# Hybrid encoder block on one core: modulation weights in column blocks, the first three w_in slabs as one group, three engines on the token tiles

## What is computed

```python
mod = jax.nn.silu(c) @ w_ada[l] + b_ada[l]                       # w_ada 1024 x 6144
sh1, sc1, gt1, sh2, sc2, gt2 = jnp.split(mod[:, None, :], 6, axis=-1)
h = rmsnorm(x, g_norm1[l]) * (1.0 + sc1) + sh1
x = x + gt1 * mixer_sublayer(h, w_in[l], ...)                    # first: z = h @ w_in, w_in 1024 x 7168
h = rmsnorm(x, g_norm2[l]) * (1.0 + sc2) + sh2
x = x + gt2 * hier_moe(h, ...)                                   # 32 experts, 2 per token
...
return rmsnorm(x, g_final)
```

## Time and profile before

| | us |
|---|---|
| median of 3 runs | 1762.74 |
| profiled execution | 1762.71 |
| its span in the trace | 1760.9 |
| PE busy | 1587.8 (90%) |
| DVE busy | 1336.4 (76%) |
| ACT busy | 682.0 (39%) |
| Pool busy | 339.0 (19%) |
| mean granted TensorE clock | 0.96 |

### The profile page before, as it was taken

The page is one execution under the profiler, slowest core; times in us unless marked ns, Lnnn a source line. Parts: engine busy times, 40 slices in busy tenths (PEclk is TensorE's granted clock), DMA queues, the critical chain, the costliest instruction groups (busy, mean ns, idle before and its releaser), DMA issues.

```text
span 1760.9 us, 21630 instructions
## 1 busy us (share of the span) xinstructions
PE 1587.8 (90%) x7040; PEld 1290.2 (73%) x7040; DVE 1336.4 (76%) x1152; ACT 682.0 (39%) x574; POOL 339.0 (19%) x208
## 2 busy tenths in 40 slices
PE   2799999999999997997989965999999999999981
PEld 2688888888888885775777854788887777777861
DVE  5687869678696878349435446999999999899984
ACT  4401121121111202214213122777776766676762
POOL 1100000000000000000000002255454444345440
PEclk9999999999999998998999975999999999999995
DMA  7413323142232315423426253999999999999945
GB/s 267 142 54 115 107 94 108 60 131 83 84 107 95 107 48 194 128 72 120 132 85 201 101 203 124 348 366 371 373 360 361 361 351 358 359 352 356 370 143 208
DMA packets 167572, 352.07 MB, mean 200 GB/s; under 512 B 17229, under 2 KB 90957, under 8 KB 167542
## 3 DMA queue, kind: packets, MB, share of 16 engines
q1 hardware_dynamic: 150838, 309.71, 49.9%
q0 software_dynamic: 16704, 41.98, 7.9%
HBM read 323.84 MB, written 46.66 MB: 210 GB/s over the span
## 4 chain that ended last, share of the span: by engine, by line
PE 59%; DMA 18%; DVE 13%; issue 4%; ACT 4%; POOL 1%; DVEq 0%; SPq 0%; POOLq 0%; ACTq 0%
PE ps L1220 18%; PE ps L1222 18%; PE ps L1221 18%; DMA e_raw<-in_w_down_dram 15%; DVE e_lo L1148 3%; ACT e_hi L723 2%; DMA xg<-d_h,g_idx 2%; DVE e_lo L1144 2%; PE ps L1276 2%; DVE macc L836 1%; PE ps L1394 1%; PE ps L1342 1%; DVE s L951 1%; DVE conf L942 1%; DVE f_o L1210 1%
## 5 line engine op out<-in xcount | busy, mean ns | idle before, releaser
L1220 PE MATMUL ps<-A_hi,w_hi 128*128 128x512 f32 x1024 | 402.9, 393 | 23.8 <-DVE A_lo L931 13.0
L1221 PE MATMUL ps<-A_lo,w_hi 128*128 128x512 f32 x1024 | 401.0, 392 | 0.0
L1222 PE MATMUL ps<-A_hi,w_lo 128*128 128x512 f32 x1024 | 400.9, 392 | 0.0
L1144 DVE TENSOR_TENSOR e_lo<-e_raw,e_hi 128x2048 fp32r<-128x2048 f32 x136 | 309.0, 2285 | 12.4 <-ACT e_hi L717 10.8
L921 DVE SCALAR_TENSOR_TENSOR conv_acc_b<-glu,colc,conv_acc_b 128x1024 f32<-128x1024 f32 x232 | 298.0, 1285 | 10.4 <-DVE rows L913 0.3
L717 ACT CAST e_hi<-e_raw 128x2048 fp32r<-128x2048 f32 x136 | 259.7, 1912 | 61.3 <-PE ps L1222 56.1
L1220 PEld LDWEIGHTS ps<-A_hi,w_hi 128*128 128x128 f32 x1024 | 194.0, 189 | 66.9 <-issue 17.8
L1221 PEld LDWEIGHTS ps<-A_lo,w_hi 128*128 128x128 f32 x1024 | 194.1, 190 | 40.7 <-issue 0.5
L1222 PEld LDWEIGHTS ps<-A_hi,w_lo 128*128 128x128 f32 x1024 | 193.8, 189 | 40.6
L1220 PE MATMUL ps<-e_hi,xT_hi 128*128 128x512 f32 x528 | 212.6, 403 | 0.0
L1222 PE MATMUL ps<-e_hi,xT_lo 128*128 128x512 f32 x528 | 206.9, 392 | 0.0
(11 more groups left out here) (227 smaller groups left out, 2025.5 us busy)
## 6 DMA issues: line engine op xcount, KB each, us to landing
e_raw<-in_w_gate_dram SPq DMA_DIRECT2D x132, 512.0 KB, 5.5
e_raw<-in_w_up_dram SPq DMA_DIRECT2D x132, 512.0 KB, 12.4
e_raw<-in_w_down_dram SPq DMA_DIRECT2D x66, 1024.0 KB, 14.0
w_raw<-in_w_in_dram SPq DMA_DIRECT2D x56, 512.0 KB, 4.3
stream<-in_w_ada_dram SPq DMA_DIRECT2D x48, 512.0 KB, 5.7
xn<-in_x_dram SPq DMA_DIRECT2D x8, 512.0 KB, 7.0
d_short<-conv_acc_a POOLq DMA_DIRECT2D x8, 512.0 KB, 4.0
d_gate_a<-gate_st POOLq DMA_DIRECT2D x8, 512.0 KB, 2.9
```

What stands on the lines that cost most here:

```text
L1144: v.tensor_tensor(e_lo[:, q, :], e_raw[:, q, :], e_hi[:, q, :].bitcast(F32), ALU.subtract).then_inc(gu_lo, 1)
L1220: t.matmul(dst, st_hi, mv_hi, start=first, stop=False)
L1221: t.matmul(dst, st_hi, mv_lo, start=False, stop=False)
L1222: return t.matmul(dst, st_lo, mv_hi, start=False, stop=last)
```

## The change

It rewrites the start; from slab 7 on the program is the same.

- **Loads.** The eight parameter loads go out on ACT's queue, `c` first. SP issues all eight x tiles, then four tiles of w_ada, then the first three w_in slabs, then the other twelve tiles of w_ada. A tile of w_ada is now 512 rows by 256 columns (four row blocks side by side in a slot, runs of 1 KB): four tiles (two row halves, shift and scale) complete 256 columns of both vectors.
- **Token tiles.** ACT squares tile i and takes the root of tile i-1; Pool scales x (was ACT); ACT copies the even transposed tiles out of PSUM, DVE the odd ones; `junk0` gets a second buffer. ACT starts no scaling and DVE no modulation sum in this loop.
- **Modulation.** DVE sums in pieces of 256 columns, 64 operations in place of 16, shift and scale in turn, each waiting for the one before the last. After each column block PE adds over the partitions (4 products) and DVE forms two columns of a1.
- **h.** Pool makes `hsc` for all eight k (was four) and the A_lo of odd k; DVE the A_lo of even k.
- **w_lo** of slabs 1 and 2 is made by Pool, of slab 0 by DVE.
- **Products.** Slabs 0, 1 and 2 run together: for each channel block k the three slabs' 18 matmuls, with the column sums of the next modulation block behind k = 0, 2 and 4. Then slab 3 and the rest as before; the first channel is written out, the loop runs over 1 to 7.

The diff, cut to its core:

```diff
+        def ada_block(m):
+            kb, kh, q = m // 4, m // 2 % 2, m % 2
+            return w_ada[kh * H:(kh + 1) * H, q * D + kb * MB:q * D + (kb + 1) * MB].rearrange("(k p) n -> p k n", p=P)
 ...
-            for src, r, n in ((conv_b, 0, KB), (conv_a, ROW_CONV_A, KA), (b_conv_b, ROW_BIAS_B, 1), (ln_g, ROW_LN_G, 1),
-                              (ln_b, ROW_LN_B, 1), (g_norm1, ROW_G1, 1), (b_ada[0:2], ROW_SH, 2), (c, ROW_C, 1)):
-                sp.dma_start(prow[r:r + n, :], src).then_inc(s_par, 16)
             for i in range(NT):
                 sp.dma_start(xn[:, i, :], x[i * P:(i + 1) * P, :]).then_inc(x_full[i], 16)
-                for q in range(2):
-                    load_tile(sp, M_ADA1 + 2 * i + q, w_ada[i * P:(i + 1) * P, q * D:(q + 1) * D])
+            def load_ada(m):
+                if m >= 4:
+                    sp.wait_ge(st_free[m % 4], m // 4)
+                sp.dma_start(tile(M_ADA1 + m).rearrange("p (k n) -> p k n", n=MB), ada_block(m)).then_inc(st_full[m % 4], 16)
+            for m in range(4):
+                load_ada(m)
+            for kind in range(3):
+                sp.dma_start(raw3[:, W_SLOT[kind]], slab_in(KINDS[kind], 0)).then_inc(wr_full[W_SLOT[kind]], 16)
+            for m in range(4, 16):
+                load_ada(m)
             sp.wait_ge(s_const, 1)
             sp.dma_start(rows[0:1, :, :], b_ada[2:6].unsqueeze(0)).then_inc(s_rows_in, 16)
-            sp.wait_ge(s_cols, 2)
-            with sp.Fori(0, KT) as ch:
+            def channel(ch, loaded):
                 for kind in range(NK):
                     s = W_SLOT[kind]
-                    held(w_lo_done, ch * NK + (kind - W_BACK[kind] + 1 + CREDIT_SLAB))
-                    sp.dma_start(raw3[:, s], slab_in(KINDS[kind], ch)).then_inc(wr_full[s], 16)
+                    if kind >= loaded:
+                        held(w_lo_done, ch * NK + (kind - W_BACK[kind] + 1 + CREDIT_SLAB))
+                        sp.dma_start(raw3[:, s], slab_in(KINDS[kind], ch)).then_inc(wr_full[s], 16)
                     if kind in (0, 2, 4, 5):
                         q = (0, 2, 4, 5).index(kind)
                         held(st_free[q], ch + M_ADA2 // 4)
                         sp.dma_start(stream[:, q, :], w_ada[bass.ds(ch * P, P), (2 + q) * D:(3 + q) * D]).then_inc(st_full[q], 16)
+            sp.wait_ge(s_cols, 2)
+            channel(0, 3)
+            with sp.Fori(1, KT) as ch:
+                channel(ch, 0)
 ...
-            pool.wait_ge(s_a1, 1)
-            for k in range(1, KT, 2):
-                if k >= 3:
-                    pool.wait_ge(s_hlo, k - 1)
-                g.tensor_scalar(hsc[:, 1, :], xnT[:, k, :], a1[:, k:k + 1], modc[:, 0, k:k + 1], ALU.mult, ALU.add).then_inc(s_hp, 1)
+            for i in range(NT):
+                pool.wait_ge(s_rstd, i + 1)
+                g.tensor_scalar(xn[:, i, :], xn[:, i, :], rstd[:, i:i + 1], None, ALU.mult).then_inc(s_xn, 1)
+            for kind in range(1, 3):
+                pool.wait_ge(w_hi_done, kind + 1)
+                s = W_SLOT[kind]
+                g.tensor_tensor(w_lo[:, s, :], w_raw[:, s, :], w_hi[:, s, :].bitcast(F32), ALU.subtract).then_inc(s_wlo_pool, 1)
+            def h_f32(k):
+                if k % 2 == 0:
+                    pool.wait_ge(s_a1, k // 2 + 1)
+                    if k >= 2:
+                        pool.wait_ge(s_hlo, k // 2)
+                g.tensor_scalar(hsc[:, k % 2, :], xnT[:, k, :], a1[:, k:k + 1], modc[:, 0, k:k + 1], ALU.mult, ALU.add).then_inc(s_hp, 1)
+            pool.wait_ge(s_xTa, NT // 2)
+            pool.wait_ge(s_xTd, NT // 2)
+            for k in range(0, KT, 2):
+                h_f32(k)
+                h_f32(k + 1)
+                pool.wait_ge(s_hp, k + 2)
+                pool.wait_ge(s_hhi, k + 2)
+                g.tensor_tensor(A_lo[:, k + 1, :], hsc[:, 1, :], A_hi[:, k + 1, :].bitcast(F32), ALU.subtract).then_inc(s_hlo_odd, 1)
+                pool.wait_ge(s_hlo_odd, k // 2 + 1)
 ...
+            for src, r, n in ((c, ROW_C, 1), (b_ada[0:2], ROW_SH, 2), (g_norm1, ROW_G1, 1), (conv_b, 0, KB), (conv_a, ROW_CONV_A, KA),
+                              (b_conv_b, ROW_BIAS_B, 1), (ln_g, ROW_LN_G, 1), (ln_b, ROW_LN_B, 1)):
+                act.dma_start(prow[r:r + n, :], src).then_inc(s_par, 16)
 ...
+            def xT_even(i):
+                act.wait_ge(s_xT, i + 1)
+                a.copy(xnT[:, :, i * P:(i + 1) * P], ps[:, i % 2, :].rearrange("p (k n) -> p k n", k=KT)).then_inc(s_xTa, 1)
 ...
             for i in range(NT):
                 act.wait_ge(x_full[i], 16)
-                a.activation(junk0[:], xn[:, i, :], ACT.Square, accum_out=ss[:, i:i + 1]).then_inc(s_ssq, 1)
-                take_root(0, i)
-                act.wait_ge(s_rstd, i + 1)
-                a.activation(xn[:, i, :], xn[:, i, :], ACT.Copy, scale=rstd[:, i:i + 1]).then_inc(s_xn, 1)
+                if i >= 2:
+                    act.wait_ge(s_ssq, i - 1)
+                a.activation(junk0[:, i % 2, :], xn[:, i, :], ACT.Square, accum_out=ss[:, i:i + 1]).then_inc(s_ssq, 1)
+                if i >= 1:
+                    take_root(0, i - 1)
+                if i >= 3 and i % 2 == 1:
+                    xT_even(i - 3)
+            take_root(0, NT - 1)
             act.sem_inc(act_evac, CREDIT_ACT_EVAC)
             for q in range(2):
                 act.sem_inc(g_free[q], CREDIT_FREE)
-            def split(n, slot, full, before):
-                act.wait_ge(wr_full[slot], full)
-                act.wait_ge(pe_slab, before)
-                a.copy(w_hi[:, slot, :], w_raw[:, slot, :]).then_inc(w_hi_done, 1)
             act.wait_ge(s_cols, 2)
-            for kind in range(2):
+            xT_even(NT - 2)
 ...
+            def mod_sum(kb, kh):
+                tiles = [M_ADA1 + kb * 4 + kh * 2 + q for q in range(2)]
                 for q in range(2):
-                    m = M_ADA1 + 2 * i + q
-                    wait_tile(dve, m)
-                    if i == 0:
-                        ins = v.tensor_scalar(macc1[:, q, :], tile(m), cols[:, i, ROW_C:ROW_C + 1], None, ALU.mult)
-                    else:
-                        ins = v.scalar_tensor_tensor(macc1[:, q, :], tile(m), cols[:, i, ROW_C:ROW_C + 1], macc1[:, q, :],
-                                                     ALU.mult, ALU.add)
-                    step(ins)
-                    dve.sem_inc(st_free[m % 4], 1)
-            dve.sem_inc(s_macc, 1)
-            xT_evac(NT - 1)
-            for kind in range(2):
-                split(W_SLOT[kind], kind + 1)
-            dve.wait_ge(s_modc, 1)
-            step(v.tensor_tensor(modc[:], ps[:, 3, 0:2 * KT].rearrange("p (q k) -> p q k", q=2),
-                                 cols[:, :, ROW_SH:ROW_SC + 1].rearrange("p k q -> p q k"), ALU.add))
-            step(v.scalar_tensor_tensor(a1[:], modc[:, 1, :], 1.0, cols[:, :, ROW_G1], ALU.add, ALU.mult))
-            dve.sem_inc(s_a1, 1)
+                    wait_tile(dve, tiles[q])
+                for j in range(4):
+                    k = kh * 4 + j
+                    ck = cols[:, k, ROW_C:ROW_C + 1]
+                    for q in range(2):
+                        acc = macc1[:, q, kb * MB:(kb + 1) * MB]
+                        src = tile(tiles[q])[:, j * MB:(j + 1) * MB]
+                        if k == 0:
+                            ins = v.tensor_scalar(acc, src, ck, None, ALU.mult)
+                        else:
+                            dve.wait_ge(dv, steps[0] - 1)
+                            ins = v.scalar_tensor_tensor(acc, src, ck, acc, ALU.mult, ALU.add)
+                        steps[0] += 1
+                        ins.then_inc(dv, 1)
+                dve.wait_ge(dv, steps[0])
+                for q in range(2):
+                    dve.sem_inc(st_free[tiles[q] % 4], 1)
+                if kh == 1:
+                    dve.sem_inc(s_macc, 1)
+            def mod_add(kb):
+                dve.wait_ge(s_modc, kb + 1)
+                two = slice(2 * kb, 2 * kb + 2)
+                step(v.tensor_tensor(modc[:, :, two], ps[:, 3, 0:2 * KT].rearrange("p (q k) -> p q k", q=2)[:, :, two],
+                                     cols[:, two, ROW_SH:ROW_SC + 1].rearrange("p k q -> p q k"), ALU.add))
+                step(v.scalar_tensor_tensor(a1[:, two], modc[:, 1, two], 1.0, cols[:, two, ROW_G1], ALU.add, ALU.mult))
+                dve.sem_inc(s_a1, 1)
+            def h_lo_even(k):
+                dve.wait_ge(s_hp, k + 1)
+                dve.wait_ge(s_hhi, k + 1)
+                v.tensor_tensor(A_lo[:, k, :], hsc[:, 0, :], A_hi[:, k, :].bitcast(F32), ALU.subtract).then_inc(s_hlo, 1)
+            mod_sum(0, 0)
+            xT_odd(5)
+            mod_sum(0, 1)
+            xT_odd(7)
+            split(W_SLOT[0], 1)
+            mod_add(0)
+            for kb in range(1, 4):
+                mod_sum(kb, 0)
+                if kb >= 2:
+                    mod_add(kb - 1)
+                else:
+                    h_lo_even(0)
```

(92 more changed lines are left out.)

47 lines of the change are left out of this document (25 added, 22 removed).

## The result

| | before | after |
|---|---|---|
| median of 4 runs each | 1763.25 us | 1784.15 us |
| ratio, 95% interval | | 1.0119, 1.0098 to 1.0141 |
| profiled execution | 1762.71 | 1783.59 |
| its span | 1760.9 | 1781.5 |
| T, start of ACT's first c_sb copy | 101.69 | 123.15 |

The account below looks back on a forecast made before the run. The chain of waits before the first w_in slabs end (T) bounds the kernel, PE being full afterwards. T = 87.6 + 5.5 + 14 = 107.1; + 2.2 - 101.7 = +7.6 us, so 1770 us, range 1751 to 1780.

Parts of the forecast that it names:

- Pool's turns: Before T, Pool's work and DVE's two-input operations exclude each other for whole operations; +14 us, between +9.6 and +18.4.
- late parameters: At the start, parameters share one DMA engine with x, halving their rate; +5.5 us, bounds 0 and +7.
- x tiles: First square to last rstd: ACT sets the pace, Pool's scalings and PE's transposes lie beside it; 18.5 us.
- strict turns: Before T, Pool and DVE alternate, so nearly all Pool's work comes on top; +18.4 us, T = 106.
- Rival 1: Pool and DVE do not block each other in two-input work; 1756 or, with prompt parameters, 1751; chance 0.25.
- one slow start: In the first channel block, PE's first matmuls start 0.43 us apart, not 0.23; +2 us.
- rival 4: PE slow again after pauses between channel blocks, up to three more starts at +2 us; 1776; 0.22 with rival 3.
- DVE's waiting for PE: Before T, 2 to 3 us of Pool's work lie under DVE's waits for PE and cost nothing.
- short sums: Modulation sums over 256 columns on DVE: 0.40 us each, 3.2 for a half block, range 0.34 to 0.48.
- +2.2: Waits of PE after the three-slab group: 1.5 us for slab 3 and 0.7 before slab 5.
- rival 3: Pool and DVE strictly in turns and parameters late; +12.0 us, 1775; chance 0.22 together with rival 4.
- 87.6: T, end of the third slab, if no engine disturbs another and parameters are prompt; range 85 to 90.

Follow-up runs that it names:

- e1: Changed kernel with the eight parameter loads on SP's queue ahead of x, in the new order; 1776.95 us.
- e7: Kernel before with the parameter loads moved to ACT's queue in the new order; 1769.38 us.
- e3: Changed kernel with Pool's scaling of x written with a second operation (plus 0.0) that changes nothing; 1777.30 us.
- e4: Changed kernel with Pool left only the scaling of x ahead of the first products; ACT writes hsc, DVE all A_lo and w_lo; 1773.53 us.
- c2: c1 with parameters on ACT's queue again and all that waits for them moved behind the x tiles; median 1748.59 us, 0.9918 of before.
- e8: e4 plus sixteen Pool operations that read and write SBUF tiles nobody uses; 1785.48 us.
- e9: As e8, but the sixteen extra Pool operations are fills that write SBUF and read nothing; T 111.9, total not given.
- e5: Changed kernel with PE's column sums issued ahead of channel blocks 2 and 4, not behind them; 1781.02 us.
- c1: Changed kernel joining e1 (parameters in before's order), e3, e4 and e5; column blocks and three-slab group kept; median 1757.62 us, 0.9968 of before.

## Why the prediction missed

The forecast of 1770 and the range up to 1780 both lie under the measured 1784. Slower by more than 0.5%, which I had given 0.34, is what came. Pool's turns and the late parameters, the two costs that I named, are there; what failed is the time of the x tiles (Pool's scaling counted as nothing), the size of the parameters' delay, and the slow restarts of PE left out of the sum.

**The account of T.** Forecast 107.1, measured 123.15, 16.0 short. By its own steps:

| step | forecast | measured | miss |
|---|---|---|---|
| first square | 17.0 | 20.86 | 3.9 |
| from it to the last rstd | 18.5 | 23.2 | 4.7 |
| from there to T | 71.6 | 79.05 | 7.4 |

- **Parameters** (+5.5): right in direction, mis-sized: the first square came 9.4 later than before's 11.49. I halved the rate and gave 15 to 16 for the last landing; it was 18.99, more than a halving (flight 15.59 against the 5.95 of the earlier trace rows), and my upper bound of 7 was under it. e1 and e7 show from both sides that the queue makes the delay; how the two queues share the engine no run shows.
- **The x tiles**: the step that failed was "Pool's scalings lie beside it". The prediction gives them no price; the only Pool row that it has is the hsc of 1.20, a two-operation form. The scaling is a one-operation form and took 2.83, longer than ACT's 1.44 a tile. PE's transposes came 2.8 apart, each waiting for Pool, and ACT's copies and roots behind them, so that Pool set the pace. With the two-operation form (e3) the stretch takes 18.1 us, my 18.5, and T falls by 7.0. No row of before shows the form, and I bounded it by nothing.
- **Pool's turns** (+14): right. Against unblocked half blocks (2.99 or 3.25, from e4 and c2) those of after lose 1.8, 4.2, 3.7, 3.5 and 3.7 us, together 16.9; the first 1.8 are beside Pool's scaling, which was not in my count, the other 15.1 beside its w_lo, hsc and A_lo, against the middle of 14 and the 18.4 of strict turns. Pool's subtraction took 2.38 to 2.42; I had said 2.3. Rival 1 (no turns in two-input work) is refuted, by e4, and by e8 against e9.
- **PE between blocks**: I priced one slow start and made three of them rival 4. There were two more before T, blocks of 18 in 6.49 and 6.61 us from the first product to the column sums (from 85.94 and from 102.68) in place of 4.1, 4.9 together. With the 2.9 by which all turns passed 14 that is 7.8, near the 7.4 of the third row, partly by luck: the three column sums took 0.8 each and not 1.7, 2.7 less, and waits and hand-overs that I had not counted are about as much more. What I had far too small is DVE's waiting for PE, 2 to 3 us in all: the column sums stand behind the block they follow, so that DVE, and with it the next block, waited (4.62 and 7.65 us). e5 removes those waits, and T falls by 7.2.
- **The short sums**: 0.41 each alone, forecast 0.40. The loads behind them cost 0.4 to 0.6 a time, within the "up to 1".

**Behind T.** Slab 3 waited 2.35 us (forecast 1.5); the wait of 0.7 for slab 5 didn't come, PE is full from 130 us on; slab 3's start was slow (0.77 for the first product). From T to the last c_sb after takes 536.8 us, before 533.1: +3.7 for my +2.2. So at the end of the slabs after is 21.5 + 3.7 = 25.2 us late, and at the end of the span 20.6. The difference lies in the experts. First gathered product, and first final output, of before:

```profile
L1394 PE MATMUL ps<-ident,xg x272: 270/283/484, 1083.6 to 1690.3; 128*128 128x128 f32 x136
```

```profile
L1210 DVE SCALAR_TENSOR_TENSOR f_o<-f_x,rstd,rows x8: 1283/1286/1286, 1738.7 to 1756.5; 128x1024 f32<-128x1024 f32 x8
```

and of after (duration ns min/median/max, first to last start):

```profile
L1522 PE MATMUL ps<-ident,xg x272: 270/283/490, 1109.7 to 1710.1; 128*128 128x128 f32 x136
```

```profile
L1306 DVE SCALAR_TENSOR_TENSOR f_o<-f_x,rstd,rows x8: 1283/1286/1286, 1759.2 to 1777.0; 128x1024 f32<-128x1024 f32 x8
```

That stage lasted 655.1 us in before and 649.5 in after, each read from one trace; the DMA share in it is 0.93 in both. It doesn't follow T: e8, with T at 121.8, took 653.3, c1 and c2 653.7, e4 651.2, e7 650.3. Part of the miss in T was thus hidden by 5.6 us of a stage that I had taken as fixed, which is luck. What moves it by this much between kernels with the same code there stays open.

**Rivals.** Rivals 3 and 4 both happened, together with the parameters' delay: each was a partial case in my list, and I gave them as alternatives (1775, 1776, at most 1781) although nothing in the trace excludes one by the other. Added up (87.6 + 5.5 + 18.4 + 6 = 117.5, +18.0 us) they would have given 1781, still 3 under the measured 1784. That is the error in the range; in the sum the errors are the scaling at nothing, the parameters at 5.5, and one slow start where there were three.

## What to carry over

Work given to an engine that is idle is not free when the two share access to SBUF: price it as a sum on the busy engine if both read (here DVE's half blocks lost 3.5 to 4.2 us beside 4.8 to 5.4 of Pool's work), and test it with a reading and a writing dummy. A price from a row holds only for the same form of the instruction, two-operation and one-operation forms included. Delays that don't exclude each other belong in one case, added; and moving waits behind the loop that can hide them (c2) brought more than moving the loads ahead.
